# A tenth place for expert weights, gather and scatter in other positions, and the last expert chunk in two transfers

## What is computed

```python
    for l in range(DEPTH):
        mix = hybrid_mixer(h, w_in[l], lower_bounds[l], hgrn_norm_g[l],
                           w_branch_sb[l], w_branch_hgrn[l], w_out[l])
        h = layer_norm(DEEPNORM_ALPHA * h + mix, ln1_g[l], ln1_b[l])
        ffn = moe(h, router_w[l], router_b[l], expert_w_up[l], expert_b_up[l],
                  expert_w_down[l], expert_b_down[l])
        h = layer_norm(DEEPNORM_ALPHA * h + ffn, ln2_g[l], ln2_b[l])
    return h
...
    def expert_block(args):
        xblk, e = args
        hcat = xblk @ w_up[e] + b_up[e]
        x_glu = jnp.minimum(hcat[:, 0::2], SWIGLU_LIMIT)
        x_lin = jnp.clip(hcat[:, 1::2], -SWIGLU_LIMIT, SWIGLU_LIMIT)
        act = x_glu * jax.nn.sigmoid(SWIGLU_ALPHA * x_glu) * (x_lin + 1.0)
        return act @ w_down[e] + b_down[e]
```

## Time and profile before

| | us |
|---|---|
| median of 3 runs | 1529.42 |
| lowest and highest of them | 1527.02, 1530.88 |
| the profiled execution's own time | 1528.25 |
| span of its trace | 1526.5 |
| PE busy in the span | 1429.0 |
| DVE busy | 584.2 |
| ACT busy | 449.3 |
| read from HBM | 514.62 MB |

### The profile page before, as it was taken

How to read it: one execution, slowest core, us unless ns; L and a number is a source line. 1 busy time by engine, 2 the same in 40 slices (tenths; PEclk the granted TensorE clock), 3 DMA queues, 4 the chain that set the end, 5 groups by cost and what they waited for, 6 DMA issues and landing times. The chain is left out here.

```text
span 1526.5 us, 19835 instructions
## 1 busy us (share of the span) xinstructions
PE 1429.0 (94%) x8005; PEld 846.0 (55%) x8005; DVE 584.2 (38%) x978; ACT 449.3 (29%) x597; POOL 38.4 (3%) x80
## 2 busy tenths in 40 slices
PE   9999999999999999988988989889889999999998
PEld 9987898344334434323423433333333788888887
DVE  4985457211210211210210210210211685777765
ACT  5654543121111112111111111111111536553343
POOL 2000030000000000000000000000000022000000
PEclk9999999999999999999999999999999999999999
DMA  8597999899999999999999999999999461345552
GB/s 284 175 295 258 327 336 411 369 427 428 427 429 427 429 428 427 430 428 428 429 428 428 429 428 428 429 428 429 428 427 367 132 193 56 108 143 191 193 188 88
DMA packets 126918, 516.47 MB, mean 338 GB/s; under 512 B 6885, under 2 KB 95310, under 8 KB 102254
## 3 DMA queue, kind: packets, MB, share of 16 engines
q1 hardware_dynamic: 125998, 513.59, 84.6%
q10 hardware_dynamic: 864, 2.10, 0.4%
HBM read 514.62 MB, written 1.05 MB: 338 GB/s over the span
## 5 line engine op out<-in xcount | busy, mean ns | idle before, releaser
L1329 PE MATMUL ps<-ring,xg 128*64 128x512 f32 x1456 | 324.8, 595 | 25.7 <-DMA ring<-in_expert_w_up 22.7
L1478 DVE TENSOR_TENSOR glu<-ps,bupT 128x512 f32<-128x512 f32 x32 | 22.1, 692 | 720.0 <-PE ps L1338 720.0
L1329 PEld LDWEIGHTS ps<-ring,xg 128*64 128x64 f32 x1456 | 102.4, 137 | 242.5 <-issue 191.5
L88 ACT ACTIVATE hrow<-ps 128x1024 f32<-128x1024 f32 x32 | 32.8, 1024 | 473.4 <-PE ps L1329 473.4
L1354 PE MATMUL ps<-ring,act 128*64 128x512 f32 x608 | 136.3, 596 | 0.0
L2221 PE MATMUL ps<-h_halves,w_hi 128*128 128x512 f32 x352 | 124.2, 399 | 0.1
L2332 DVE TENSOR_TENSOR w_lo<-ring,w_hi 128x2048 fp32r<-128x2048 f32 x36 | 82.5, 2292 | 55.8 <-ACT w_hi L88 55.8
L1329 PE MATMUL ps<-more,xg 128*64 128x512 f32 x416 | 93.0, 595 | 8.7 <-DMA more<-in_expert_w_up 7.5
L2226 PE MATMUL ps<-h_halves,w_lo 128*128 128x256 f32 x348 | 97.7, 281 | 0.0
L88 ACT ACTIVATE w_hi<-ring 128x2048 fp32r<-128x2048 f32 (+1 forms) x38 | 70.8, 1865 | 70.8 <-PE ps L2226 34.6
L88 ACT ACTIVATE y<-ps 64x512 f32<-64x512 f32 x64 | 37.9, 592 | 182.0 <-PE ps L1354 181.6
(11 more groups left out here) (419 smaller groups left out, 2256.4 us busy)
## 6 DMA issues: line engine op xcount, KB each, us to landing
ring<-in_expert_w_up SPq DMA_DIRECT2D x91, 2048.0 KB, 36.8
ring<-in_expert_w_down SPq DMA_DIRECT2D x38, 2048.0 KB, 39.3
more<-in_expert_w_up SPq DMA_DIRECT2D x26, 2048.0 KB, 35.4
more<-in_expert_w_down SPq DMA_DIRECT2D x16, 2048.0 KB, 38.8
ring<-in_w_in SPq DMA_DIRECT2D x28, 1024.0 KB, 8.3
ring<-in_w_ada SPq DMA_DIRECT2D x24, 1024.0 KB, 5.8
x_xT_xn<-in_expert_w_up SPq DMA_DIRECT2D x11, 2048.0 KB, 36.8
ring<-in_w_gu SPq DMA_DIRECT2D x22, 1024.0 KB, 5.1
```

The source lines that it names most:

```text
L88: return nc.scalar.activation(out, x, ACT.Copy)
L1329: last = nc.tensor.matmul(up[a2 * CAP:(a2 + 1) * CAP, u, :], k.xg[:, q, h * CAP:(h + 1) * CAP], w[:, c:c + 512], start=(q == 0), stop=(q = ...
L1478: link(nc.vector.tensor_tensor(k.glu[:, :, :, :], g, b[:, 0].to_broadcast(wide), ALU.add))
```

## The change

A tenth place is made of two parts of SBUF, and each chunk that falls to it comes in two transfers of 1 MB (8 KB in a row on each partition). The loop holds 5 pairs and runs 3 times. The second half of a gather moves into up(0) of its own pair, behind two of its four chunks; the scatter moves behind up(1), and turn(1) between the two chunks of down(0). The last of all chunks comes in two transfers with a count of its own for the first (`k.last_half`); the loads for what follows wait for that count. Both tiles of the running sum are added by PE. The diagonal matrices go, and `gate_rows` multiplies a broadcast column with the identity instead. The transposes of the gates and the first gather move from `branches` to `experts`, behind the count of rounds. In `second_mix`, `projection(0)` waits tile by tile.

```diff
-PLACES = 9
+PLACES = 10
-EXTRA, MORE = 5, 7
+EXTRA, MORE, SPLIT = 5, 7, 9
-LOOPED = 3
+LOOPED = 5
...
-            for i in (MORE, MORE + 1):
+            for i in (MORE, MORE + 1, SPLIT):
                 load_expert(k, sp, a, 0, i)
...
+def gate_rows(nc, k, row, banks):
+    for m in range(KD):
+        last = nc.tensor.matmul(k.ps[:, banks[m // 4], (m % 4) * P:(m % 4 + 1) * P],
+                                k.mod[:, row + m:row + m + 1].to_broadcast([P, P]), k.ident[:, :], start=True, stop=True)
...
+    if place == SPLIT or halves:
+        for half, dst in enumerate(expert_chunk(k, place)):
+            landed = halves[half] if halves else k.expert_in[place]
+            sp.dma_start(dst, src[:, half * 2048:(half + 1) * 2048]).then_inc(landed, 16)
...
             done = extra * (E * PER)
+            sp.wait_ge(k.last_half, extra * 16 + 16)
             sp.wait_ge(used, done + place_free(EXTRA))
...
-            gather(nc, k, 5, range(4, KD)).then_inc(g_done, 1)
+            pe.wait_ge(k.gate_ready, 1)
+            for t in range(TT):
+                last = nc.tensor.transpose(turned[0:E, 0, t * P:(t + 1) * P], k.gate[:, t, :], k.ident[:, :])
+            last.then_inc(gT_done, 1)
             extra = extra_rounds(pe)
...
                 for q in range(KD):
+                    if h == 0 and q == 4:
+                        pe.wait_ge(acc_done, n * 2 + 1)
+                        gather(nc, k, 5, range(4, KD)).then_inc(g_done, 1)
...
                 units_turned(n, 0)
+                up_weights(r, turn, at, n, 1)
                 pe.wait_ge(selT_ready, n + 1)
                 pe.wait_ge(y_ready, n * 2 + 1)
                 pe.wait_ge(k.bias_in, 32)
-                scatter()
-                pe.wait_ge(acc_done, n * 2 + 3)
-                up_weights(r, turn, at, n, 1)
                 pe.wait_ge(act_ready, n * 2 + 1)
+                scatter(between)
+                down_weights(r, turn, at, n, 0, (0,))
+                pe.wait_ge(acc_done, n * 2 + 4)
                 units_turned(n, 1)
-                down_weights(r, turn, at, n, 0)
+                down_weights(r, turn, at, n, 0, (1,))
...
                 if tail:
-                    pe.wait_ge(act_ready, n * 2 + 2)
-                    gather(nc, k, 3, range(KD // 2)).then_inc(g_done, 1)
                     down_weights(r, turn, at, n, 1, (0,))
-                    gather(nc, k, 3, range(KD // 2, KD)).then_inc(g_done, 1)
-                    down_weights(r, turn, at, n, 1, (1,))
+                    pe.wait_ge(selT_ready, n + 2)
+                    sum_so_far(0)
+                    down_weights(r, turn, at, n, 1, (1,), True)
...
-            dve.wait_ge(acc_done, extra * (2 * pairs) + (2 * pairs + 1))
-            collect(0)
-            dve.wait_ge(acc_done, extra * (2 * pairs) + (2 * pairs + 3))
             for half in range(2):
-                ins = nc.vector.bn_stats(k.stats[:, 0, half, :], k.acc[:, 0, half * 512:(half + 1) * 512])
+                ins = nc.vector.bn_stats(k.stats[:, 0, half, :], final[0][:, half, :])
...
+            def tile_turned(t):
+                pe.wait_ge(hT_ready, 4 + t + 1)
+                pe.wait_ge(hT_front, t + 1)
...
+            act.wait_ge(gT_done, 1)
+            act_copy(nc, k.selT[0:E, :], turned[0:E, 0, 0:T]).then_inc(selT_ready, 1)
             extra = extra_rounds(act)
             nc.scalar.activation(k.trig[:, :, :], k.ang[:, :, :], ACT.Sin).then_inc(k.trig_ready, 1)
...
-            pe.wait_ge(hT_ready, 4 + 2 * TT)
             projection(0)
```

More of the change, by code:

```diff
@@ L331, in feature_major, with token_major @@
     return last
-def token_major(nc, out, w, xT, kt, n):
+def token_major(nc, out, w, xT, kt, n, wait):
     for t in range(TT):
+        wait(t)
         for q in range(kt):
@@ L962, in logits @@
                 return last
-            def gate_row(half):
-                return nc.tensor.matmul(k.ps[:, half, :], k.ones[:, :], k.diag[0][:, half * 512:(half + 1) * 512],
-                                        start=True, stop=True)
             for c in range(2):
@@ L1022, in _ @@
                 .then_inc(pos_done, 1)
-            pe.wait_ge(gate_ready, 1)
-            for t in range(TT):
-                last = nc.tensor.transpose(k.ps[0:E, 6, t * P:(t + 1) * P], k.gate[:, t, :], k.ident[:, :])
-            last.then_inc(gT_done, 1)
-            pe.wait_ge(k.hot_ready, 1)
-            gather(nc, k, 5, range(4)).then_inc(k.g_done, 1)
         @blk.scalar
@@ L1423, in pair @@
             def pair(n, tail):
+                gathered(n, 1, rows[:, 1, :])
                 for h in range(2):
@@ L1784, in _ @@
             high(5)
+            act.wait_ge(k.gb_done, 1)
+            for half in range(2):
+                act_copy(nc, k.gB[:, 1, half * 512:(half + 1) * 512], k.ps[:, 4 + 3 * half, :])
             evacuate(2)
@@ L2151, in turned @@
                             ins.then_inc(done, 1)
-            for half in range(2):
-                last = nc.tensor.matmul(k.ps[:, 6 + half, :], k.ones[:, :], k.diag[1][:, half * 512:(half + 1) * 512],
-                                        start=True, stop=True)
-            last.then_inc(k.gb_done, 1)
-            fill(nc, k, 4, k.gB[:, 0, 0:512], 1)
+            gate_rows(nc, k, GATE1, (6, 7)).then_inc(k.gb_done, 1)
+            fill(nc, k, 4, k.bupT[:, 0:512], 1)
             turned(mixed, mn, mt)
@@ L2489, in program @@
                           for n in ("in_hi", "in_lo"))
+        base = nc.sbuf_base
+        with nc.sbuf_tensor("under", [P, TENTH_AT], F32), nc.sbuf_tensor("tenth", [P, SLOT], F32) as v:
+            k.tenth = v[:, :]
         with ExitStack() as early:
@@ L2565, in program @@
                 first_mix(nc, k, a)
-                k.diag = [k.x[:, n, :] for n in range(2)]
                 branches(nc, k, a)
```

188 lines of the change are left out of this document (101 added, 87 removed).

## The result

| | median, us | runs | profiled execution | its span |
|---|---|---|---|---|
| before, on the same chip | 1528.27 | 1525.40 to 1530.88 (5) | | 1526.5 |
| after | 1538.72 | 1536.41 to 1538.81 (5) | 1538.72 | 1537.2 |

A forecast was written before the change was run, and what follows sets the result against it. The prediction took the expert weight stream at about 428 GB/s as the bound, with gains only at its start, in its rate or behind it. Terms summed to -2.75 us: 1526.7 from a median of 1529.42, range 1523.3 to 1529.8.

The forecast's parts named there:

- The loop of five pairs, +1.4: Expert loop: the larger body is fetched again every turn, 24 more instruction packets at about 0.08 us each.
- rival (d): Expert stream: instruction packets all pass one DMA engine, 0.61 us each, so +10.5 us, 1539.9; chance 8%.
- TensorE's clock, taken as 0: Opening: the forecast's sum counted no fall of TensorE's granted clock; only a rival did.
- Rival (b): Opening: TensorE's granted clock falls once, first release 1.7 us later, total -1.05 us, 1528.4; chance 13%.
- The first release, +1.3: Opening: ACT's longer chain ahead of its first copy delays PE's first expert product and the stream by 1.3 us.
- in the loop this is worth nothing: Expert loop: moving gather and scatter gains nothing, as a pair near 54 us hides under 58.8 us of transfers.
- The tail, −0.9 and −0.25: Behind the stream: PE's last down product comes 0.9 us earlier, and the block then ends another 0.25 us earlier.
- −0.5 for `projection(0)`: Behind the block change: starting `projection(0)` tile by tile removes PE's idle 0.50 us.
- rival (c): Behind the stream: held-back loads come 1.5 us later than worked out and the norms wait; -1.25 us, 1528.2; chance 8%.
- just used up: Behind the block change: ACT's 1.1 us of slack just covers the later `in_w_in`; taken as 0.
- Rows of 8 KB, +1.1: Expert stream: 19 chunks in 8 KB rows lose a third of what 4 KB rows lose, 1.1 us.
- The tenth place, −4.9: Stream's start: one chunk fewer is left when the stream restarts, gaining 4.9 us.

The follow-up runs named there:

- e3: The kernel before with its expert loop written out to fifteen pairs in one turn instead of three pairs a turn; 1534.93 us, ratio 1.0041.
- e6: e5 with its loop of three pairs written out to fifteen pairs in one turn; 1536.62 us.
- e1: The changed kernel with two fill products of 256 columns at each of three places of PE's opening; 1533.73 us, ratio 1.0042.
- e5: The changed kernel with nine places, three pairs in the loop and the opening fills of e1; 1531.26 us.
- e13: The changed kernel with nine places, gathers and gate transposes placed as in the kernel before, and four fills in the opening; 1528.03 us.
- e14: e13 with, in the last pair alone, the scatter earlier and half of tile 0's sum in the wait for `y`; 1526.55 us.
- e8: e5 with tile 0's scatter ahead of the second expert's up products and tile 1's behind their first chunk; 1532.11 us, ratio 1.0017.
- e10: e9 with the early scatter of e8; 1530.98 us.
- e4: The kernel before with every chunk through its nine places fetched by two transfers of 1 MB instead of one; 1543.89 us, ratio 1.0100.
- e7: e5 with every chunk of the ninth place (21 of 192) fetched by two transfers of 1 MB; 1533.28 us.
- e12: e11 with ten places and five pairs in the loop again; 1532.45 us.
- e11: e10 without the wait that holds the later loads back; 1530.66 us.
- e9: e5 with more fills in the opening and the sine of the angles moved to the old block; 1530.08 us.

## Why the prediction was wrong

The prediction had −2.75 us; the runs show +10.5. Its range was also added up too short: the forecast with 2.1 us for rows of 4 KB and 1.7 for the clock is 1530.5, not 1529.8, which changes nothing here. Its account of what bounds the kernel held: each part acted through the stream's start, its rate or what lies behind it. Four terms failed.

**The loop of five pairs, +1.4: the price of a packet.** That every turn fetches again was right (33 packets between 300 and 1130 us instead of 5; 24 more were expected). The Trainium skill (Runtime: NRT & Kernel Launch, Instruction fetch mechanics) gives PE a buffer of 128 KiB, by which 96 KB stay in reach and 160 KB do not, and the traces agree: the earlier trace rows shows no packet in a later turn of before, the rows of after 8 in 140 us. The same section of the Trainium skill says that a taken branch whose target lies outside the current window of two pages forces a fetch; by this the 96 KB of before would be fetched again too, and they are not. Wrong was the 0.08 us a packet, from the weights missing in one stretch. It is the part that missing bytes explain (e3 and e6 show 0.09), and a mean rate cannot show that chunks land late with equal bytes moved. e3 and e6 measure 4.1 to 6.5 us for 24 packets, 0.17 to 0.27 each. This is rival (d) in its direction, at or beyond its turning point of 0.17, though not at its 0.61, and its one DMA engine is not shown; the sentence that 0.08 "speaks against it" is, with the clock, the error that cost most.

**TensorE's clock, taken as 0.** The change took the gate products out of PE's opening, and the prediction counted this nowhere as a loss. Rival (b) had the mechanism and priced it at 1.7 us, for a fall of 3.4 us. The fall lasted 16 us and covered logits, position products, gather and the first expert products: 4.6 us of delay at the refill, 3 to 5 at the end, which e1 took away with fills alone. The argument against it, that the clock had not fallen with shorter waits, compared idle times; what had changed was also the work between them.

**The first release, +1.3.** With the clock held the first refill is 1.0 us later against the logits (e1: 19.4 us instead of 18.4), so this chain was sized well. But "in the loop this is worth nothing" was applied to the first pair too, where the stream waits for PE: with the gather inside `up(0)` the third and fourth refill come 9.8 and 13.3 us behind the first (e5), before 6.8 and 10.3. By 1160 us about 0.9 us of that is left (0.4 against -0.5 in the table, e5 and e13); with ten places it was not measured alone.

**The tail, −0.9 and −0.25.** Behind the fourth up chunk PE needed 26.1 us to the last product, not 24.0. Most parts were short: five chunks at 3.6 instead of 3.44 (0.7), `y`'s copy that the gather used to hide (1.1), scatter and sum (0.4). And the scatter went from a place with slack, ahead of chunks that PE must wait for, to one without (1.2 us idle at each of those chunks in after). e14 puts it back in the last pair: PE's tail ends 2.8 us earlier against the logits, and the median is 1.5 us lower. The −0.25 for the block end was right (from the last product's end to the block change 6.6 instead of 6.85), and so was −0.5 for `projection(0)` (−0.67). The held-back loads were in time, as predicted, and rival (c) did not occur; it appears as soon as PE's tail is shortened (e8, e10, e14: ACT waits 1.9 to 2.0 us for `in_w_in`), as "just used up" said.

**Rows of 8 KB, +1.1,** was nearly right: 0.08 to 0.10 us a chunk (e4, e7), 1.5 to 2.0 us for 19 chunks. It was a third of a bound read from one window of 4 KB rows, so this is in part luck. **The tenth place, −4.9,** was right as a head start: e10 and e12, with the same first refill (19.1 us behind the logits), moved 16.60 and 18.74 MB from 252 to 300 us, 5.0 us apart. But in this kernel it came with the other two.

The account against the forecast: clock 3 to 5, fetches 2.7 to 5.1 (4.1 to 6.5 less the 1.4 counted), chunks 0.4 to 0.9, tail 2.1 make 8 to 13 of the 13.2 us between forecast and result. The single runs of one kernel lie up to 7 us apart (e11), so the rest can't be assigned.

## What to carry to other kernels

A buffer more at the start of a stream is a one-time gain; whatever it forces on the loop (more code per turn, smaller transfers) is paid through the whole stream, so price those first. Where chunks gate the work, a mean rate is not enough: compare when the chunk arrives with how many bytes have arrived. And before moving work off an engine or out of a gap, ask at both ends of the stream which side waits there: the same move can be free in the steady state and cost in the first and the last round.

## What the runs showed of the hardware

- An instruction packet of 16 KB among weight transfers at 428 GB/s cost 0.17 to 0.27 us (e3, e6), several times its bytes' 0.04 us. About 0.09 us of it are missing bytes (354.45 MB in e6 against 355.40 in e5, 24 packets more). Another part shows with equal bytes moved: e6 got its chunk 2.3 us later than e5. That this is unevenness between DMA engines is inferred from a DMA share near 0.5; which of them carry the packets the profile does not show.
- Fetching chunks in two transfers of 1 MB with rows of 8 KB instead of one of 2 MB with rows of 16 KB cost 1.5% of the rate (e4: 59.05 MB against 59.97 in 140 us).
- The granted clock of TensorE fell in after near 259 us, behind idle times of 0.34, 0.76 and 0.47 us with small products between them, and stood at 0.50 (1.2 GHz) for 16 us. With one and the same opening it fell in one profiled execution (e9) and not in three others (e10, e11, e12).
- A loop of PE of three pairs, about 96 KB as the prediction counts it, was not fetched again in later turns (no packet from 480 to 620 us); one of five pairs, about 160 KB, was (8 packets there).
